# A hybrid encoder trunk: the mixers' values turned by VectorE and DMAs instead of TensorE

## The reference

```python
for i in range(DEPTH):                                  # 2
    hn = _rms(h, norm_mix[i])
    if i % 2 == 0:                                      # 8 attention heads of 128, 4 mLSTM heads of 128/256
        h = h + _even_mixer(hn, ...)                    # h @ w_in, both mixers, y @ w_out
    else:                                               # GLA: 4 heads, keys 256, values 512, chunks of 64
        h = h + _odd_mixer(hn, ...)
    h = h + _conv_ffn(_rms(h, norm_ffn[i]), ...)        # up 2 x 5632, depthwise conv of 3, silu gate, down
return h[:, N_META:]
```

```python
bcum = jnp.cumsum(log_a, axis=2)
decay = jnp.exp(jnp.where(tri[:, :, None], bcum[..., :, None, :] - bcum[..., None, :, :], -jnp.inf))
a = jnp.einsum('bhtd,bhsd,bhtsd->bhts', q, k, decay)
```

## Time and profile before

| | us |
|---|---|
| median of 3 runs (lowest, highest) | 2303.25 (2301.75, 2305.57) |
| profiled execution, its own time | 2301.8 |
| span of that execution | 2300.1 |
| PE busy | 2292.2 |
| DVE busy | 1624.5 |
| ACT busy | 1200.8 |
| POOL busy | 93.2 |

### The profile page before, as it was taken

One profiled execution on the slowest core, in us unless ns is written; L12 is line 12 of the kernel. 1 busy time (PEld: TensorE's weight loads), 2 busy tenths in 40 slices (PEclk: granted clock), 3 DMA queues, 4 the chain that ended last, 5 costly groups with the idle time before them and its releaser, 6 DMA issues.

```text
span 2300.1 us, 50383 instructions
## 1 busy us (share of the span) xinstructions
PE 2292.2 (100%) x19184; PEld 2254.2 (98%) x19184; DVE 1624.5 (71%) x2373; ACT 1200.8 (52%) x1705; POOL 93.2 (4%) x152
## 2 busy tenths in 40 slices
PE   9999999999999999999999999999999999999999
PEld 9999999999999999999999999999999999999998
DVE  6677676777756775677587867877777567767775
ACT  7567566644434453444477555456554444444443
POOL 1010121000000000000021010000000000000000
PEclk9999999999999999999999999999999999999999
DMA  7555665566665566656566544566666656566565
GB/s 227 165 157 165 161 169 163 177 190 193 193 191 183 181 196 187 186 182 199 190 179 186 156 121 137 155 192 187 191 201 202 202 181 212 185 208 196 185 208 167
DMA packets 432019, 420.34 MB, mean 183 GB/s; under 512 B 26178, under 2 KB 431084, under 8 KB 431884
## 3 DMA queue, kind: packets, MB, share of 16 engines
q1 hardware_dynamic: 418620, 415.56, 58.4%
q10 hardware_dynamic: 13264, 2.90, 1.1%
HBM read 416.31 MB, written 2.10 MB: 182 GB/s over the span
## 4 chain that ended last, share of the span: by engine, by line
PE 99%; DVE 0%; DMA 0%; issue 0%; SPq 0%; ACT 0%; DVEq 0%; ACTq 0%
PE ps L1842 31%; PE ps L1840 28%; PE ps L1841 28%; PE ps L1838 6%; PE ps L2104 1%; PE ps L1931 1%; PE ps L1932 1%; PE ps L2098 0%; PE ps L2058 0%; PE ps L1977 0%; DMA tok<-in_x 0%; PE ps L2016 0%; PE ps L1935 0%; PE ps L2156 0%; PE ps L1908 0%
## 5 line engine op out<-in xcount | busy, mean ns | idle before, releaser
L1840 PE MATMUL ps<-act_hi,w_hi 128*128 128x272 f32 (+1 forms) x4864 | 1359.1, 279 | 0.2 <-issue 0.2
L1842 PE MATMUL ps<-act_hi,w_lo 128*128 128x272 f32 (+1 forms) x4864 | 1348.8, 277 | 0.0
L1841 PE MATMUL ps<-act_lo,w_hi 128*128 128x272 f32 (+1 forms) x4864 | 1348.8, 277 | 0.0
L1210 DVE TENSOR_TENSOR w_lo<-raw,w_hi 128x1024 fp32r<-128x1024 f32 (+1 forms) x799 | 947.1, 1204 | 437.0 <-ACT w_hi L676 413.0
L676 ACT ACTIVATE w_hi<-raw 128x1024 fp32r<-128x1024 f32 (+1 forms) x796 | 814.0, 1035 | 633.7 <-PE ps L1842 607.0
L1840 PEld LDWEIGHTS ps<-act_hi,w_hi 128*128 128x128 f32 x4864 | 923.4, 190 | 3.3 <-issue 1.4
L1841 PEld LDWEIGHTS ps<-act_lo,w_hi 128*128 128x128 f32 x4864 | 923.5, 190 | 0.7
L1842 PEld LDWEIGHTS ps<-act_hi,w_lo 128*128 128x128 f32 x4864 | 923.3, 190 | 0.0
L1842 PE MATMUL ps<-g_both,w_lo 128*128 128x272 f32 (+1 forms) x1408 | 388.4, 276 | 0.0
L1842 PEld LDWEIGHTS ps<-g_both,w_lo 128*128 128x128 f32 x1408 | 268.2, 190 | 0.0
L1838 PE MATMUL ps<-g_both,w_hi 128*128 128x512 f32 x676 | 222.2, 383 | 0.0
(11 more groups left out here) (349 smaller groups left out, 1217.1 us busy)
## 6 DMA issues: line engine op xcount, KB each, us to landing
raw<-in_ffn_w_up SPq DMA_DIRECT2D x352, 512.0 KB, 4.6
raw<-in_ffn_w_down SPq DMA_DIRECT2D x128, 512.0 KB, 4.4
raw<-in_c_w_in SPq DMA_DIRECT2D x96, 512.0 KB, 3.9
raw<-in_ab_w_in SPq DMA_DIRECT2D x95, 512.0 KB, 3.9
raw<-in_ffn_w_down SPq DMA_DIRECT2D x64, 384.0 KB, 3.9
raw<-in_ab_w_out SPq DMA_DIRECT2D x32, 512.0 KB, 3.8
raw<-in_c_w_out SPq DMA_DIRECT2D x32, 512.0 KB, 4.4
tok<-in_x SPq DMA_DIRECT2D x8, 256.0 KB, 6.9
```

The lines of the kernel that those rows point to most:

```text
L1210: V.tensor_tensor(w_lo[:, s % 4, 0:kc * 256], raw[:, s % 4, 0:kc * 256], w_hi[:, s % 4, 0:kc * 256].bitcast(F32), ALU.subtract).then_inc(S ...
L1840: mm(o, wh, moving(xh, kk), start=(c == 0 and k == 0), stop=False)
L1841: mm(o, wh, moving(xl, kk), start=False, stop=False)
L1842: ins = mm(o, wl, moving(xh, kk), start=False, stop=end)
```

## The change

1. *Values.* `vt` keeps the transpose of the meta tokens and `vt_copy` the copies of them. The 256 other tokens of a pair of tiles (128 x 512) are turned by DVE within each block of 32 x 32 (`turn_values`) into new buffers, in the ticks of `V_TURN` (even layer) and `GL_TURN` (GLA). One tick later ACT issues four DMAs that write them to DRAM in pieces of 32 elements, at the place where each block belongs (`turn_out`). Four ticks behind the turn (five in GLA) ACT waits for these and issues two DMAs that read 128 x 256 each back into `v_tok` (`turn_back`); `weigh` waits for them. DVE has waits for `v_out` at ticks that write over the buffers.
2. *Meta keys.* Step 0 only copies its inputs into `ko` and `ka`; the scans and the product stand behind the step with H = 2.
3. *Wide weights.* The mLSTM scores and the sums of squares of the meta tile use 128 weight columns in place of 16, the rest going to rows that nobody reads.
4. *Opening.* Two warm-up matmuls fewer; the third pair's `turn_in` stands behind the first group of matmuls; ACT's and DVE's first operations stand in another order.

```diff
+        V_TURN = {17: 0, 18: 1, 29: 2, 31: 3, 77: 4, 81: 5, 85: 6, 89: 7}
+        GL_TURN = {4 * (k + 1): 8 + k for k in range(8)}
+        v_turns = nc.dram_tensor("v_turns", (16, 2 * SEQ, P), F32, kind="Internal").ap()
...
# vt (TensorE) and weigh
-                tr(pm[b][0:META, 2 * P:3 * P], src[:, 0:META], ident[:, :])
-                tr(pm[b][:, 0:P], src[:, META:META + P], ident[:, :])
-                tr(pm[b][:, P:2 * P], src[:, META + P:T], ident[:, :]).then_inc(S("vt_done"), 1)
+                tr(pm[b][0:META, 2 * P:3 * P], src[:, 0:META], ident[:, :]).then_inc(S("vt_done"), 1)
+            def weigh(o, v0, ptt, ptm, low, tile):
+                q = tile // 2
+                pe.wait_ge(v_back[q % 2], 32 * (q // 2 + 1))
...
# DVE
+            def turn_values(q, src):
+                V.transpose(turned(q).rearrange("p (a t) -> p a t", a=2), src[:, :, META:T]).then_inc(S("v_turned"), 1)
...
# ACT: vt_copy, then the new functions
-                A(v_tok[:, 1:3, c:c + P], strided(pm[b], [[P, 2], [1, P]]), ACT.Copy).then_inc(S("vt_copied"), 1)
+            def turn_out(q):
+                act.wait_ge(S("v_turned"), q + 1)
+                v = v_turns[q]
+                for c in range(4):
+                    dst = bass.AP(v.tensor, v.offset + 32 * c, [[P, 32], [32 * P, 16], [1, 32]])
+                    act.dma_start(dst, turned(q)[32 * c:32 * c + 32, :].rearrange("p (b j) -> p b j", j=32)).then_inc(v_out[q % 2], 16)
+            def turn_back(q):
+                act.wait_ge(v_out[q % 2], 64 * (q // 2 + 1))
+                if q >= 2:
+                    act.wait_ge(v_back[q % 2], 32 * (q // 2))
+                v = v_turns[q]
+                for j in range(2):
+                    c = VT_COL[2 * q + j]
+                    src = bass.AP(v.tensor, v.offset + j * SEQ * P, [[P, P], [P * P, 2], [1, P]])
+                    act.dma_start(v_tok[:, 1:3, c:c + P], src).then_inc(v_back[q % 2], 16)
...
# ACT, GLA ticks (the even layer has t - 1 and t - 4), ahead of the tick's own work
+                    if t - 1 in GL_TURN:
+                        turn_out(GL_TURN[t - 1])
+                    if t - 5 in GL_TURN:
+                        turn_back(GL_TURN[t - 5])
...
# DVE, GLA step(): unit 0, and behind the step with H == 2
-                        meta_keys(hd, a, lk)
+                        V.tensor_copy(ko[:, hd % 2, :, :], lk[:, :, 0:META])
+                        V.tensor_copy(ka[:, :, 0:Q0 - 1], a[0][:, :, 1:Q0])
...
+                    if H == 2:
+                        meta_keys(hd)
...
# TensorE, even layer
-                        mm(pm[2][0:tn, 0:T], proj[:, 24 + hd, t0:t0 + tn], proj[:, 28 + hd, :], start=True, stop=True).then_inc(S("ml_scores"), 1)
+                        mm(pm[2][:, 0:T], proj[:, 24 + hd, t0:t0 + P], proj[:, 28 + hd, :], start=True, stop=True).then_inc(S("ml_scores"), 1)
-                            ins = mm(pm[3][0:tn, c:c + 1], x_, ones[:, 0:1], start=True, stop=True)
+                            ins = mm(pm[3][:, c:c + 1], x_, ones[:, 0:1], start=True, stop=True)
...
# opening
+        TURN_AFTER = {0: (2,), 1: (3, 4), 2: (5,), 3: (6,), 4: (7,)}
-            warm(4)
+            warm(2)
-            turn_in(2)
```

More of the change, by code:

```diff
@@ L234, in build @@
         tail_r = sb("tail_r", [P, T], F32R, at=M + 3 * TB)
+        ml_turn = sb("ml_turn", [P, 4, 2 * SEQ], at=zone + 8 * TB)
+        na_turn = sb("na_turn", [P, 2, 2 * SEQ], at=M + 2 * TB)
+        gl_turn = sb("gl_turn", [P, 8, 2 * SEQ], at=zone + 32 * TB)
         ge = sb("ge", [P, 2, 2, T], at=zone + 40 * TB)
@@ L277, in S @@
             return names[name]
+        v_out = [S(f"v_out{j}") for j in range(2)]
+        v_back = [S(f"v_back{j}") for j in range(2)]
         landed = [S(f"weights_landed{j}") for j in range(4)]
@@ L282, in build @@
             sq_ready sq_added ss_ready rt_ready rs_ready x_hi act_ready n_ready tail_high tail_split tail_done tail_evac
-            vt_done vt_copied qk_sq qk_ss qk_rt qk_ready rq_rt bias_ready
+            vt_done vt_copied v_turned qk_sq qk_ss qk_rt qk_ready rq_rt bias_ready
             na_scores na_biased na_max na_exp na_norm na_ptdone na_ptcopied na_pv na_stored mask_done tail_added
@@ L852, in even @@
                         vt_copy(n, b)
+                    if t - 1 in V_TURN:
+                        turn_out(V_TURN[t - 1])
+                    if t - 4 in V_TURN:
+                        turn_back(V_TURN[t - 4])
                     if t == 1:
@@ L1240, in evac @@
                         dve.wait_ge(S("vt_done"), 16 + 2 * gi - 2)
+                        dve.wait_ge(S("v_turned"), 8 + gi - 1)
                     V.tensor_tensor(ntmp[:, 2 * (gi % 2):2 * (gi % 2) + 2, :], banks, rs, ALU.mult).then_inc(S("bank_free"), 1)
@@ L1492, in even @@
                 for t in range(EVEN_TICKS):
+                    if t in V_TURN:
+                        q = V_TURN[t]
+                        dve.wait_ge(S("bank_free"), 2 + 4 + q + 1 if q < 4 else 2 + G["na_in"]["gr0"] + 8 + q - 4 + 1)
+                        if q == 4:
+                            dve.wait_ge(S("qk_ss"), NA_HEADS)
+                        if q in (6, 7):
+                            dve.wait_ge(v_out[q % 2], 64 * 3)
+                        e = E_ML[2 * q] if q < 4 else E_NA[2 * q - 8]
+                        turn_values(q, proj[:, e:e + 2, :])
+                    if t == 36:
+                        for sem in v_out:
+                            dve.wait_ge(sem, 64 * 2)
                     if t == 4:
@@ L1590, in gla, with meta_keys @@
                 V.memset(km[:, :], 0.0)
-                def meta_keys(hd, a, lk):
-                    o = ko[:, hd % 2, :, :]
+                def meta_keys(hd):
+                    o = ko[:, hd % 2, :, 0:Q0 - 1]
                     for j in range(2):
[L1596 to L1599, removed]
+                        ins = V.tensor_tensor_scan(ka[:, j, 0:Q0 - 1][:, ::-1], ka[:, j, 0:Q0 - 1][:, ::-1], ones[:, 0:Q0 - 1], 1.0,
+                                                   ALU.mult, ALU.mult)
+                    link(ins)
+                    V.tensor_tensor(o, o, ka[:, :, 0:Q0 - 1], ALU.mult)
                 def meta_rows(hd, rq, lk):
@@ L1700, in gla @@
                             step(steps.index(units[u]))
+                    if t in GL_TURN:
+                        q = GL_TURN[t]
+                        dve.wait_ge(S("bank_free"), 2 + G["v_in"]["gr0"] + q - 8 + 1)
+                        turn_values(q, ntmp[:, 2 * (q % 2):2 * (q % 2) + 2, :])
+                    if t == 35:
+                        dve.wait_ge(v_out[0], 64 * 8)
+                        dve.wait_ge(v_out[1], 64 * 7)
+                    if t == 39:
+                        dve.wait_ge(v_out[1], 64 * 8)
                     if t in MAKE:
@@ L1735, in first_half, with fill_even @@
                                 ALU.subtract).then_inc(S("split_done" if b else "split_half"), 1)
-            first_half(0)
+            def fill_even(p):
+                b = PAIR_BANK[p]
+                V.tensor_copy(h[:, 2 * p:2 * p + 2, META:T], ps[:, b:b + 2, 0:SEQ]).then_inc(S("h_dve"), 1)
             dve.wait_ge(S("par_evac"), 1)
+            first_low(0)
             dve.wait_ge(S("meta_done"), 1)
@@ L1750, in _ @@
                                     ALU.subtract).then_inc(S("meta_ready"), 1)
+                if p == 1:
                     first_half(1)
+                if p == 1:
+                    fill_even(0)
                 if p in (1, 3, 5):
                     lo(gemms[0], 0, (p + 1) // 2)
-                if p % 2 == 0:
-                    b = PAIR_BANK[p]
-                    V.tensor_copy(h[:, 2 * p:2 * p + 2, META:T], ps[:, b:b + 2, 0:SEQ]).then_inc(S("h_dve"), 1)
+                if p % 2 == 0 and p:
+                    fill_even(p)
             lo(gemms[0], 0, 4)
@@ L1844, in body @@
                                 ins.then_inc(S("last_used"), 1)
-                            if opening and j % 4 == 3 and 2 * s + j // 4 + 3 < KT // 2:
-                                turn_in(2 * s + j // 4 + 3)
+                            if opening and j % 4 == 3:
+                                for p in TURN_AFTER.get(2 * s + j // 4, ()):
+                                    turn_in(p)
                         ins.then_inc(S("used"), 1)
```

23 lines of the change are left out of this document (14 added, 9 removed).

## The result

The changed kernel takes 2314.11 us in the median of 6 runs (2310.96 to 2314.81), the kernel before 2303.53 (6 runs): a ratio of 1.0048, 95% interval 1.0038 to 1.0058. The forecast was 2298.3, its range up to 2307.0. The profiled execution ran 2313.2 us, its span is 2311.2.

A forecast was written before the change was run, and what follows sets the result against it. TensorE, busy 2292.2 of 2300.1 us, was taken to bound the kernel; 7.0 + 0.8 + 0.1 + 2.0 = 9.9 us gained less 5.0 given back by ACT's issues made 4.9, so 2298.3 us, range 2293 to 2307.

The forecast's parts named there:

- Transposes: TensorE's value tiles: 64 transposes fewer at 0.109 us each, 7.0 us gained, all on the path.
- Wide scores: Four mLSTM meta scores on TensorE, widened from 16 to 128 weight columns: 0.8 us gained.
- One-column matmuls: Widened matmuls of L2016 on TensorE: faster narrow step and cost of width change taken as equal, 0, ends -0.7 and +0.7.
- Opening: Kernel start, fewer warm-up matmuls and new order: 0.1 us gained, ends 0 and 1.
- DVE's blocks: Sixteen DVE transposes of 128x512, 0.7 us each, 11 us in all, costing 0 because DVE sits idle before them.
- Meta keys put off: GLA head 2: scans miss GpSimd, TensorE's km and kc waits shrink; 2.0 us gained, ends 0.9 and 2.7.
- D: Time ACT spends on six DMA issues in one GLA tick: 2.9 us, ends 2.4 and 3.8, or 4.3 with one blocked.
- its formula: GLA ticks 17, 21, 25: TensorE's kc stall is six-issue time less 1.4 us, giving 1.5 us each.
- I count it once, 0.5, ends 0 and 3: Even layer: four ACT issues, 1.9 us, ahead of a result as tight as kc would cost 0.5 us.
- the GLA one: TensorE waiting for kc behind ACT's issues at GLA ticks 17, 21 and 25: 4.5 us given back.
- Transfers: Turn DMAs land before turn_back needs them, over 8 us later in even layer, over 11 in GLA: ACT does not wait.
- Rival (2): ACT's queue bounds at the kc ticks: 15 us given back, 2308 us, or 2303 with issues totalling 3.8; chance 0.18.

The follow-up runs named there:

- e2b: Kernel before with the change's meta keys, wide weights and opening, but values' transposes and copies as before: 2301.14 us, ratio 0.9991.
- e6: Changed kernel with the even layer's value turns issued by GpSimd, GLA's still by ACT: 2306.13 us, ratio 1.0011.
- e4b: Changed kernel with all turn_out and turn_back DMAs issued by GpSimd at the same ticks, behind v_low: 2295.85 us, ratio 0.9968.
- e8: Changed kernel with value turns and bias loads issued by GpSimd and the opening of the kernel before: 2304.94 us, ratio 1.0009.
- e3b: Changed kernel with turn_out and turn_back moved to the end of their ACT ticks in both layers: 2308.04 us, ratio 1.0016.
- e7: Changed kernel with GLA's turn_back one tick later, so no ACT tick has all six issues: 2308.13 us, ratio 1.0021.
- e1b: Changed kernel without its 96 DMAs, ACT copying DVE's turned blocks straight into v_tok (values not the reference's): 2295.46 us, ratio 0.9966.
- e5: Changed kernel with the 32 attention bias loads issued by GpSimd, value turns still by ACT: 2309.99 us, ratio 1.0033.

## Why the prediction was wrong, point by point

- *Transposes*, 7.0: measured 7.0 (19,116 instructions, not 19,118: a warm-up matmul counts as two). *Wide scores*, 0.8: measured 0.7. *One-column matmuls*, 0, ends -0.7 and +0.7: 0.9, just outside. *Opening*, 0.1: 0.4 in the profiled execution of the change, 0.45 lost in that of e2b, so not resolved.
- *DVE's blocks*, 0.7 each: right, as DVE's groups in the changed kernel have it. Nothing on the path: right but for tick 17. There ACT's first issue waits for DVE's turn and starts 0.04 us behind its end, 1.02 us behind ACT's first copy (1331.47), where in tick 21 the two are 0.29 apart:

```profile
L1533 DVE STREAM_TRANSPOSE gl_turn<-ntmp 128x512 f32<-128x512 f32 x8 | 5.7, 708 | 0.1
```

```profile
1331.75 0.70 DVE L1533 STREAM_TRANSPOSE gl_turn<-ntmp 128x512 f32<-128x512 f32 x1
...
1332.49 0.33 ACTq L856 DMA_DIRECT2D v_turns<-gl_turn  x1
```

  A put-off `meta_keys` stands just ahead of this turn (1331.36 to 1331.84), so "TensorE does not wait for it" is not quite right either.

- *Meta keys put off*, 2.0 (0.9 to 2.7): 0.6 in e2b, below its lower end. The scans do run in 0.17 us now, but the sum took the cause to be the scan and it was the place. The copy `ko` is held in its stead, 1.27 us. The text had this as a condition, with 0.9 as its end. The Trainium skill (SBUF — State Buffer, on SBUF's two separate sides) names the cause, a port pair held for a whole instruction; the rows above agree with it for plain copies and for the weight split.
- *D*, the six issues of a GLA tick, 2.9 us (2.4 to 4.3): the seven bursts took 3.60, 3.07, 3.06, 3.14, 3.64, 3.93 and 3.29. The prediction lets issuing start 0.31 us behind the first copy (1358.15, and 1358.06 less 0.22); at ticks 17, 21 and 25 it started 1.02, 0.29 and 0.44 us behind it. With D and start as measured its formula gives 2.4, 1.7 and 2.4; measured are 2.38, 1.70 and 2.35 (the idle time and the 0.16 that a row outlasts a step). So the mechanism, its place and its size were right within 2 us: 6.4 for 4.5 us, and 0.9 more behind the bursts of ticks 9 and 29.
- **The step that failed** is "I count it once, 0.5, ends 0 and 3" for the even layer: 8.6 us by e6. It took an issue there at 0.48 as well, and a burst as four of them alone; in tick 86 the four took 4.65 us, behind two bias issues of 3.33. The row read for its median, 630 ns, had 2177 as its highest; that one started at 308.2 and landed at 317.8, in the same stretch, and how busy the DMA engines are there does not enter the prediction. The kernel before has, from 310 to 320 us, columns as above:

```profile
310.00:320.00 10.00, 10.00 (x82) 9.55 (x82) 6.53 (x15) 6.94 (x21) 2.22 (x3) 1.00 0.79 195
```

  By the ratios the result is 16.0 us above the forecast: 8.1 of them are this term, 5.4 the GLA one (9.9 for 4.5, low clock included), and 2.5 lie in the gains (7.4 by e4b, for 9.9).

- *The clock* was no term at all. In the profiled execution of the change two low stretches follow stalls. The stalls of ticks 86 and 25 are 5.91 and 2.35 us, and what they delay is 7.6 and 4.1 (steps of the side-by-side): 1.7 us more each.
- *Transfers*: ACT never waited for `v_out`. The Trainium skill's read-modify-write below 512 B (DMA: Bandwidth & Descriptors, Specifications) was weighed against this change; a `turn_out` landed in 3.3 to 4.7 us in the median, and no run here shows that it cost anything.
- *Rival (2)* named the mechanism and had 0.18. Its price ended at 2308 because it shared these faults: one blocked issue for a burst, 3 us for the even layer, and no clock.

In sum, from the two profiled executions: gained are 7.0 + 0.7 + 0.9 (the scores and the sums of squares) + 0.4 (opening) + 1.2 (the two GLA stalls, the first here 0.9) = 10.2; lost are 10.1 in the even layer and 9.4 in GLA, low clock included, and 1.7 for the low stretch near 69 us that the profiled execution of before happens not to have: 21.2. The difference, 11.0, is that of the spans, 11.1, but for 0.1.

## What to carry to other kernels

A DMA issue is an instruction of the engine that issues it: when work moves from the engine that bounds the kernel to transfers, ask which sequencer issues them, what stands behind the issue, and give them to an engine that nobody waits for, as many as it has time for (96 in e4b, not 128 in e8). Price an issue by the highest value in its row and by how busy the DMA engines are in that stretch, not by its median. And when a slow instruction is to be moved away from where another engine holds it up, expect the next one to be held there.

## What the runs showed of the hardware

- The same issue of 64 KB by ACT took 0.31 to 2.19 us, a bias load 0.60 to 3.42. Those over 1.6 us lie between 305 and 346 us, where the DMA share is 0.56 to 0.84 by stretches of 10 us (0.87 from 322 to 328) and weight chunks issued at 317.8 and 320.9 landed in 10.8 and 9.8 us in place of 4. GpSimd's issues of the same transfers took 0.65 to 0.82 in all stages of e4b. The cause of ACT's blocking inside the DMA system was not taken apart, and one rival to the load of the engines stands untested, the backlog of ACT's own queue. In the traces of the kernel before, of the change and of e3b to e7, from 40 us on, ACT issued 105 times with none of its own DMAs under way, and none of these issues took over 0.71 us; every one over 1.1 us found one to seven of its own under way.
- Over the traces of the change and of e1b to e8 the clock went to its lower level during 12 of the 15 stalls of TensorE longer than 2 us or just behind them. Near the shorter ones it did so only in the opening of e3b and e5, at the end of a wait of 1.4 us, and near 69 us it does so with no stall ahead; so no rule follows from the length of a stall. Where TensorE has work in such a stretch it does half of it, so the wait of 2.35 us in tick 25 cost 4.1.
- DVE's `transpose` of 128x512 float32 within 32x32 blocks takes 0.70 us. With it and with GpSimd's issues the values come into token order for 7 us less of TensorE's time, and of new waits e4b has one of 1.2 us for `pt` and one of 0.3 for `pt_r`. Its 0.9968 of the kernel before holds the change's other parts too, which alone are 0.9991 (e2b).
